# Rotary embedding without TensorE products: row-exchanged copies on ScalarE, cosine, sine and sum on GpSimd

## The chip, the cores and the metric

The kernel runs on one core of a Trainium2 chip. The metric is the device time of one execution in microseconds, lower is better. The engines are TensorE (PE in the rows, with its weight loads as PEld), VectorE (DVE), ScalarE (ACT), GpSimd (POOL) and SyncE (SP), which issues most of the transfers.

## The reference

Two transformer-like blocks on 256 tokens of width 1024, in float32. What matters here is the input projection of each block, and the rotary embedding of some of its columns:

```python
def rope(x, pos):                      # block one; _rope of block two is the same
    half = HEAD_DIM // 2               # 32
    ...
    x1, x2 = xf[..., :half], xf[..., half:]
    return jnp.concatenate([x1 * c - x2 * s, x2 * c + x1 * s], axis=-1)
...
# block one, beside an RWKV-7 recurrence over the same projection
z = u @ w_in[i]
qkv = z_attn.reshape(B, S, 3, N_GROUPS, ATTN_HEADS_PER_GROUP, HEAD_DIM)
q = rope(qkv[:, :, 0], pos)            # 768 columns
k = rope(qkv[:, :, 1], pos)            # 768 columns
# block two: rope on q_b, q_idx, q_c (256 columns each), k_b, k_idx, k_cmp, k_sel, k_win (64 each)
```

In block one q and k go into a dilated attention; RWKV-7 runs beside it. In block two the rotated columns go into a top-k attention, its index scores, and an attention with compressed, selected and windowed keys.

## The kernel before

All work is written out by hand, engine by engine. Five programs (`sync_program`, `tensor_program`, `scalar_program`, `vector_program`, `gpsimd_program`) walk through the same generators. A yield is a place where a `Turns` object switches between a main stream and a side stream; the order of each engine's instructions is fixed when the program is built. Engines meet only at semaphores: each `Count` (`rope_act`, `rope_pool`, ...) is one, `up(...)` raises it and `at(...)` is the value to wait for.

**Weights.** A stream (`st1` for block one, `st2` for block two) brings weight slots, 1 MB each as a rule, into a ring of three. The load of slot j waits until TensorE has finished slot j-3. Each product is made from a high and a low part: ScalarE writes the high part of a slot's two halves (`split(st, j, (0,))` and `split(st, j, (1,))`, rows `parts<-low 128x1024` on ACT), VectorE subtracts to get the low part (rows `parts<-low,parts` on DVE, line 2710), and TensorE waits for the low part (`parted`) of each half. With these parts it computes z by features, 256 columns a chunk (`feature_chunk`, lines 807, 808 and 816: 2 x 24 matmuls of 256 columns), or by tokens (`token_range`, lines 721 to 723). Feature chunks alternate between PSUM banks 0 and 1, and ScalarE reads a finished bank before the chunk after next may write it.

**Rotary embedding.** Here z of a chunk stands as features by tokens, 128 rows being two heads, so the partner of a row is 32 rows away. ScalarE copies z to SBUF (`rope_read`), TensorE multiplies the copy by the constant matrix `C_ROT` (ones and minus ones) one chunk later (`rotate`, line 766), and VectorE multiplies the product by sine (line 2783). In block one VectorE also makes the cosine product out of PSUM (line 2816) and the sum (line 2822). In block two GpSimd makes the cosine product (line 3701) and the sum (line 3706).

**Block one, chunks 10 to 15 of `st1`** are q and k, called n = 0 to 5. They are the main stream; RWKV is the side stream: `strict` (lines 1132 on TensorE, 2964 to 2971 on VectorE), then the levels of `chain` (lines 1192 to 1225 on TensorE, 3002 on VectorE, and copies out of PSUM on ScalarE). In order_1, between chunk n = 1 and chunk n = 2 TensorE has the first level's products (lines 1192, 1195, 1145), and within chunk n = 2 the products of line 1217. The scores of the attention (line 1346) wait for the last rotated chunk.

**Block two.** Plan n = 0 and 1 are head chunks without rotation. n = 2 to 6 are slots j = 0 to 4 of `st2`: n = 5 has four pieces of 64 columns, n = 6 has only 128 columns. Slots 5 and 6 hold 464 columns by tokens (`token_range`, `read_vt`), in five pieces each. That range writes first the bank of chunk n = 5 (token half i = 0), then the bank of chunk n = 6 (i = 1). After chunk n = 6 ScalarE copies rotated keys to other rows (`high<-high 64x256`, three of them), which waits for the sum of n = 5.

ScalarE's side of a chunk:

```python
for n in range(steps):
    if n < 2:
        split(st, j + 1, (n,))
    yield
q.wait_ge(*main_pe.at(st.tag, j, 1))
read()
yield
```

and `split` itself waits for the slot's transfer (`landed`) and for TensorE's end of slot j-2.

## Time and profile before

| | us |
|---|---|
| median of 3 runs | 912.58 (911.99 to 912.64) |
| the profiled execution, its own time | 912.49 |
| its span, first to last instruction | 910.7 |
| outside the span | 1.8 |
| TensorE busy in the span | 890.3 (98%) |
| VectorE busy | 604.7 (66%) |
| ScalarE busy | 454.3 (50%) |
| GpSimd busy | 44.3 (5%) |

The granted clock of TensorE is 0.998 of full speed (2.4 GHz) over the span. Busy time of TensorE counts pipelined matmuls, so a busy TensorE says that there is no gap, not that it runs at its peak. The chain that ended last says which engine's work set the end at each place.

### The profile page before, as it was taken

Reading aid. Unit: us, or ns where it says so; the run is one execution under the profiler, and the core shown is the slowest. Engines: PE = TensorE matmul, PEld = TensorE weight load, DVE = VectorE, ACT = ScalarE, POOL = GpSimd, SP = SyncE. Lnnn points to the kernel's source line nnn. Section 1 sums busy time; section 2 is a strip of 40 time slices with the busy share of each in tenths; the row PEclk is TensorE's granted clock in tenths of the full one; section 3 lists DMA queues with packets and bytes.
Section 4 is the critical chain, followed back from the end, with each engine's and each line's share of the span. In section 5 each row is a group of like instructions: output and inputs, shape, how many; then the busy total and the mean of one; then the engine's idle time right before and its main releaser. Section 6 shows DMA issues by size and latency. Waiting matters only on the chain.

```text
span 910.7 us, 15439 instructions
## 1 busy us (share of the span) xinstructions
PE 890.3 (98%) x6574; PEld 752.5 (83%) x6574; DVE 604.7 (66%) x966; ACT 454.3 (50%) x731; POOL 44.3 (5%) x61
## 2 busy tenths in 40 slices
PE   7999999999899999999999999999999999999997
PEld 5999988787789888888889978776788788888885
DVE  4577978557766666656766477877863566666673
ACT  4775444346443444546544356484622545555561
POOL 0010000010000000000000440000000000000000
PEclk9999999999999999999999999999999999999999
DMA  9544333233578665555339574353817566665521
GB/s 341 186 139 140 97 100 110 72 95 117 206 254 278 185 185 187 189 202 203 108 130 222 137 223 145 127 186 96 276 44 208 141 188 189 192 192 192 200 95 47
DMA packets 131205, 150.78 MB, mean 166 GB/s; under 512 B 11808, under 2 KB 102176, under 8 KB 131008
## 3 DMA queue, kind: packets, MB, share of 16 engines
q1 hardware_dynamic: 129920, 145.57, 51.6%
q10 hardware_dynamic: 1216, 4.23, 1.2%
q8 instruction: 52, 0.85, 0.4%
q14 instruction: 17, 0.14, 0.0%
HBM read 148.73 MB, written 1.05 MB: 164 GB/s over the span
## 4 chain that ended last, share of the span: by engine, by line
PE 90%; DVE 4%; ACT 2%; issue 2%; DMA 1%; POOL 0%; POOLq 0%; ACTq 0%; DVEq 0%
PE psum L834 12%; PE psum L721 10%; PE psum L723 9%; PE psum L722 9%; PE psum L839 7%; PE psum L807 4%; PE psum L808 4%; PE psum L816 4%; PE psum L787 4%; PE psum L727 3%; PE psum L883 2%; PE psum L893 2%; PE psum L884 2%; PE psum L840 2%; PE psum L1724 2%
## 5 line engine op out<-in xcount | busy, mean ns | idle before, releaser
L1827 ACT ACTIVATE parts<-low 128x1024 fp32r<-128x1024 f32 (+3 forms) x252 | 254.3, 1044 | 66.3 <-PE psum L723 50.2
L2710 DVE TENSOR_TENSOR parts<-low,parts 128x1024 fp32r<-128x1024 f32 (+3 forms) x156 | 187.9, 1234 | 27.6 <-ACT parts L1827 27.4
L721 PE MATMUL psum<-parts 128*128 128x512 f32 (+2 forms) x424 | 169.4, 399 | 1.8 <-DVE parts L2710 1.0
L723 PE MATMUL psum<-parts 128*128 128x512 f32 (+2 forms) x424 | 163.5, 386 | 0.0
L722 PE MATMUL psum<-parts 128*128 128x512 f32 (+2 forms) x424 | 163.4, 385 | 0.0
L1827 ACT ACTIVATE high<-psum 128x512 f32<-128x512 f32 (+4 forms) x95 | 52.4, 562 | 162.0 <-PE psum L840 76.4
L834 PE MATMUL psum<-parts 128*128 128x512 f32 x462 | 116.8, 392 | 0.0
L834 PEld LDWEIGHTS psum<-parts 128*128 128x128 f32 x462 | 86.9, 188 | 16.9
L721 PEld LDWEIGHTS psum<-parts 128*128 128x128 f32 x424 | 79.6, 188 | 23.3 <-issue 4.0
L723 PEld LDWEIGHTS psum<-parts 128*128 128x128 f32 x424 | 79.6, 188 | 16.3
L722 PEld LDWEIGHTS psum<-parts 128*128 128x128 f32 x424 | 79.8, 188 | 14.2 <-issue 0.2
L2775 DVE TENSOR_TENSOR parts<-low,parts 128x1024 fp32r<-128x1024 f32 x54 | 66.0, 1222 | 35.3 <-ACT parts L1827 35.3
L807 PE MATMUL psum<-parts 128*128 128x256 f32 (+2 forms) x312 | 82.3, 300 | 0.0
L808 PE MATMUL psum<-parts 128*128 128x256 f32 (+2 forms) x312 | 76.8, 282 | 0.0
L839 PEld LDWEIGHTS psum<-parts 128*128 128x128 f32 x528 | 72.0, 190 | 5.1
L839 PE MATMUL psum<-parts 128*128 128x256 f32 x528 | 73.6, 282 | 0.0
L807 PEld LDWEIGHTS psum<-parts 128*128 128x128 f32 (+2 forms) x312 | 58.9, 189 | 4.1 <-issue 3.2
L808 PEld LDWEIGHTS psum<-parts 128*128 128x128 f32 (+2 forms) x312 | 59.0, 189 | 2.3 <-issue 2.2
L3206 DVE TENSOR_TENSOR mid<-psum,high 128x512 f32<-128x512 f32 x33 | 22.8, 691 | 46.2 <-ACT high L1827 46.2
L816 PE MATMUL psum<-parts 128*128 128x256 f32 (+2 forms) x312 | 43.8, 283 | 0.0
L3669 POOL TENSOR_TENSOR low<-low 128x1 f32<-128x1 f32 x20 | 11.0, 550 | 632.3 <-DVE low L2634 316.2
L816 PEld LDWEIGHTS psum<-parts 128*128 128x128 f32 (+2 forms) x312 | 40.0, 189 | 0.1
(317 smaller groups left out, 1340.0 us busy)
## 6 DMA issues: line engine op xcount, KB each, us to landing
low<-in_w_in_dram SPq DMA_DIRECT2D x40, 1024.0 KB, 5.3
low<-in_w_ffn_in_dram SPq DMA_DIRECT2D x44, 512.0 KB, 5.2
low<-in_w_ff_in_dram SPq DMA_DIRECT2D x16, 1024.0 KB, 5.9
low<-in_w_ff_out_dram SPq DMA_DIRECT2D x16, 1024.0 KB, 4.9
low<-in_w_ffn_out_dram SPq DMA_DIRECT2D x11, 1024.0 KB, 4.9
low<-in_w_out_dram SPq DMA_DIRECT2D x8, 1024.0 KB, 5.3
low<-in_w_ple_gate_dram SPq DMA_DIRECT2D x4, 1024.0 KB, 4.9
low<-consts_dram ACTq DMA_DIRECT2D x1, 2142.0 KB, 9.0
```

What stands on the lines that cost most here:

```text
L721: mm(o, l[0], r[0], start, False)
L722: mm(o, l[0], r[1], False, False)
L723: return mm(o, l[1], r[0], False, stop)
L787: t = mm(PSUM[0:m, banks[n], 256 * j + 128 * i:256 * j + 128 * i + 128], w3[:, k, off:off + m], uT[:, k, 128 * i:128 * i + 128], k == 0, k ...
L807: mm(o, hi[:, k, c], st.uh[:, k, :], k == 0, False)
L808: mm(o, lo_[:, k, c], st.uh[:, k, :], False, False)
L816: t = mm(o, hi[:, k, c], st.ul[:, k, :], False, k == 7)
L834: mm(p, hi[:, k, c], st.u2(k), k == 0, False)
L839: mm(p[:, 0:256], lo_[:, k, c], st.uh[:, k, :], False, False)
L1827: return e.activation(o, a, ACT.Copy)
L2710: tt(rslot3(n, nk, width)[:, r, 0:w], slot3(n, nk, width)[:, r, 0:w], st.hi3(j)[:, r, 0:w].bitcast(F32), ALU.subtract) \
L2775: tt(rview(OR + 2048 * n + 1024 * (k % 2), 1024), slot(n)[:, 1024 * (k % 2):1024 * (k % 2) + 1024], rview(base, 1024).bitcast(F32), ALU.su ...
```

## The change

1. The constant `C_ROT` goes, and with it TensorE's rotation (`rotate`, line 766) of all eleven rotated chunks, and VectorE's products and sums (lines 2783, 2816, 2822).
2. ScalarE writes, besides the plain copy of z, a second copy with 32-row blocks exchanged (`swapped`: four copies of 32 rows out of PSUM) straight into the place of the result.
3. GpSimd multiplies the plain copy by cosine, the exchanged copy by sine (the sign now lies in the sine table) and adds them, in block one too. Its first product waits for the plain copy only.
4. ScalarE's copy of a chunk waits for GpSimd's sum of two chunks before; the bank comes free after the fourth exchanged copy; the scores of block one wait for GpSimd's last sum.
5. In block two the first half's split of slots 2 to 6 is issued right after the wait for the chunk's end and ahead of the chunk's copies (`ahead`), not behind them.

```diff
-            def rotate(tag, n, m, z):
-
-                b = 2 + n % 2 if tag == "qk" else 5 + n % 3
-                p = bank(b)
-                q.wait_ge(*rope_act.at(tag, n))
-                mm(p[:, 0:256 * m], const(C_ROT, 128), z, True, True).then_inc(rope_pe.up(tag, n), 1)
-                free[b] = [rope_dve.at(tag, n)]
...
-                        q.wait_ge(*rope_dve.at("qk", 5, "sum"))
+                        q.wait_ge(*rope_pool.at("qk", 5))
...
+            def ahead(st, j):
+
+                return st.tag == "st2" and 2 <= j <= 6
+
             def feature_chunk(st, j, widths, read):
                 steps = 1 + len(widths)
                 for n in range(steps):
-                    if n < 2:
+                    if n == 1 or n == 0 and not ahead(st, j + 1):
                         split(st, j + 1, (n,))
                     yield
                 q.wait_ge(*main_pe.at(st.tag, j, 1))
+                if ahead(st, j + 2):
+                    split(st, j + 2, (0,))
                 read()
                 yield
...
+            def swapped(dst, z):
+
+                for p in range(4):
+                    t = copy(dst[32 * p:32 * p + 32], z[32 * (p ^ 1):32 * (p ^ 1) + 32])
+                return t
+
-            def rope_read(tag, n, m, b, zs):
+            def rope_read(tag, n, m, b, zs, dst):
                 if n >= (2 if tag == "qk" else 4):
-                    q.wait_ge(*(rope_pe.at(tag, n - 2) if tag == "qk" else rope_pool.at(tag, n - 2)))
-                copy(zs, halves(bank(b))[:, 0:m, :]).then_inc(rope_act.up(tag, n), 1)
+                    q.wait_ge(*rope_pool.at(tag, n - 2))
+                z = halves(bank(b))[:, 0:m, :]
+                copy(zs, z).then_inc(rope_act.up(tag, n, "z"), 1)
+                swapped(dst, z).then_inc(rope_act.up(tag, n), 1)
...
-            def cosines(n, b):
-                q.wait_ge(*rope_act.at("qk", n))
-                tt(rt1[n % 2], halves(bank(b)), rep(const(C_COS, 256), 2), ALU.mult).then_inc(rope_dve.up("qk", n, "cos"), 1)
-
-            def rotate1(n):
-                dst = qk[:, 2 * n:2 * n + 2, :]
-                rotate("qk", n, 2, dst, const(C_SIN, 256))
-                q.wait_ge(*rope_dve.at("qk", n))
-                tt(dst, dst, rt1[n % 2], ALU.add).then_inc(rope_dve.up("qk", n, "sum"), 1)
...
-            def rope(tag, n, m, zs, t1, cos):
+            def rope(tag, n, m, zs, dst, cos, sin):
+                q.wait_ge(*rope_act.at(tag, n, "z"))
+                tt(zs, zs, rep(const(cos, 256), m), ALU.mult).then_inc(rope_pool.up(tag, n, "cos"), 1)
                 q.wait_ge(*rope_act.at(tag, n))
-                tt(t1, zs, rep(cos, m), ALU.mult).then_inc(rope_pool.up(tag, n, "cos"), 1)
-
-            def rotate(tag, n, dst, t1):
-                q.wait_ge(*rope_dve.at(tag, n))
-                q.wait_ge(*rope_pool.at(tag, n, "cos"))
-                tt(dst, dst, t1, ALU.add).then_inc(rope_pool.up(tag, n), 1)
+                tt(dst, dst, rep(const(sin, 256), m), ALU.mult).then_inc(rope_pool.up(tag, n, "sin"), 1)
+                q.wait_ge(*rope_pool.at(tag, n, "sin"))
+                tt(dst, dst, zs, ALU.add).then_inc(rope_pool.up(tag, n), 1)
```

**VectorE in block one**, from the end of `strict` to the second group of low parts (line numbers shift by 5 to 20 between the kernels). Before:

```order
61 L2971 TENSOR_TENSOR high<-high,low 64x512 x2
62 L2971 TENSOR_TENSOR mid<-high,low 64x512
63 L2971 TENSOR_TENSOR high<-high,low 64x512
64 L2816 TENSOR_TENSOR mid<-psum,low 128x512
65 L2783 TENSOR_TENSOR mid<-psum,low 128x512
66 L2822 TENSOR_TENSOR mid<-mid 128x512
67 L2710 TENSOR_TENSOR parts<-low,parts 128x1024 x2
68 L2816 TENSOR_TENSOR mid<-psum,low 128x512
69 L3002 TENSOR_TENSOR high<-psum,low 64x512 x4
```

Of the changed kernel, the same place:

```order
61 L2951 TENSOR_TENSOR high<-high,low 64x512 x2
62 L2951 TENSOR_TENSOR mid<-high,low 64x512
63 L2951 TENSOR_TENSOR high<-high,low 64x512
64 L2705 TENSOR_TENSOR parts<-low,parts 128x1024 x2
65 L2982 TENSOR_TENSOR high<-psum,low 64x512 x4
66 L2958 TENSOR_TENSOR high<-psum,low 128x4x128 x2
```

The low parts of the next slot now follow the four products of `strict` directly, and the products of the first level follow these.

**ScalarE in block one**, around chunks n = 0 and 1 (`mid<-psum 128x512` is the plain copy of q or k, `high<-psum` are RWKV's copies). Before:

```order
60 L1827 ACTIVATE mid<-psum 128x512
61 L1827 ACTIVATE parts<-low 128x1024
62 L1827 ACTIVATE high<-psum 128x512
63 L1827 ACTIVATE parts<-low 128x1024
64 L1827 ACTIVATE high<-psum 128x512
65 L1827 ACTIVATE mid<-psum 128x512
66 L1827 ACTIVATE parts<-low 128x1024 x2
```

Of the changed kernel:

```order
60 L1808 ACTIVATE mid<-psum 128x512
61 L1808 ACTIVATE mid<-psum 32x512 x4
62 L1808 ACTIVATE parts<-low 128x1024
63 L1808 ACTIVATE high<-psum 128x512
64 L1808 ACTIVATE parts<-low 128x1024
65 L1808 ACTIVATE high<-psum 128x512
66 L1808 ACTIVATE mid<-psum 128x512
67 L1808 ACTIVATE mid<-psum 32x512 x4
68 L1808 ACTIVATE parts<-low 128x1024 x2
```

Four copies of 32 rows stand between the plain copy and the next slot's splits.

**ScalarE in block two**, from the end of chunk n = 4 to the second token slot (`128x928` are halves of slots 5 and 6). Before:

```order
268 L1827 ACTIVATE high<-psum 128x512
269 L1827 ACTIVATE parts<-low 128x928 x2
270 L1827 ACTIVATE high<-psum 128x256
271 L1827 ACTIVATE high<-high 64x256 x3
272 L1827 ACTIVATE parts<-low 128x928 x2
```

Of the changed kernel:

```order
278 L1808 ACTIVATE parts<-low 128x928
279 L1808 ACTIVATE high<-psum 128x512
280 L1808 ACTIVATE high<-psum 32x2x256 x4
281 L1808 ACTIVATE parts<-low 128x928 x2
282 L1808 ACTIVATE high<-psum 128x256
283 L1808 ACTIVATE high<-psum 32x256 x4
284 L1808 ACTIVATE high<-high 64x256 x3
285 L1808 ACTIVATE parts<-low 128x928
```

The first halves of slots 5 and 6 now stand ahead of the copies of chunks n = 5 and n = 6; the second half of slot 5 stands behind five copies of n = 5 in place of one.

## Rows read from the trace of the kernel before

**Rows 1.** The page: busy time by engine.
```profile
PE 890.3 (98%) x6574; PEld 752.5 (83%) x6574; DVE 604.7 (66%) x966; ACT 454.3 (50%) x731; POOL 44.3 (5%) x61
```

**Rows 2.** Windows: busy us of each engine (instructions), clock, DMA share, GB/s.
```profile
84.00:100.00 16.00, 16.00 (x236) 15.10 (x235) 12.60 (x23) 8.13 (x13) 0.00 (x0) 1.00 0.43 133
100.00:112.00 12.00, 11.94 (x267) 10.70 (x266) 11.06 (x14) 4.66 (x7) 0.00 (x0) 1.00 0.29 90
112.00:152.00 40.00, 39.88 (x948) 34.99 (x948) 31.00 (x44) 16.89 (x26) 0.00 (x0) 1.00 0.35 108
500.00:532.00 32.00, 31.43 (x219) 28.32 (x218) 17.59 (x15) 12.76 (x19) 18.68 (x17) 1.00 0.72 193
```

**Rows 3.** Line 766, the rotations: min/median/max ns, first and last start.
```profile
L766 PE MATMUL psum<-mid,low x12: 590/590/594, 94.3 to 148.2; 128*128 128x512 f32 x12
L766 PE MATMUL psum<-high,low x10: 378/590/594, 502.9 to 527.1; 128*128 128x512 f32 x8, 128*128 128x256 f32 x2
```

**Rows 4.** The chain that ended last, pieces: start, us, what.
```profile
94.49 0.86 PE psum L766 x2
...
524.42 3.17 DVE parts L2710 x2
527.63 0.48 PE psum L721
```

**Rows 5.** Timeline of VectorE in block one: start, us, instruction.
```profile
95.79 1.41 DVE L2971 TENSOR_TENSOR high<-high,low 64x512 f32<-64x512 f32 x2
...
98.67 0.69 DVE L2816 TENSOR_TENSOR mid<-psum,low 128x512 f32<-128x512 f32 x1
...
100.60 2.35 DVE L2710 TENSOR_TENSOR parts<-low,parts 128x1024 fp32r<-128x1024 f32 x2
...
103.47 2.84 DVE L3002 TENSOR_TENSOR high<-psum,low 64x512 f32<-64x512 f32 x4
```

**Rows 6.** Timeline of TensorE in block one.
```profile
102.65 0.38 PE L807 MATMUL psum<-parts 128*128 128x256 f32 x1
...
106.55 0.27 PE L1217 MATMUL psum<-high 64*64 64x64 f32 x1
...
153.73 0.94 PE L1346 MATMUL psum<-mid 64*128 64x128 f32 x12
```

**Rows 7.** Timeline of ScalarE in block one.
```profile
93.10 0.60 ACT L1827 ACTIVATE mid<-psum 128x512 f32<-128x512 f32 x1 [4.65 <-PE psum L816]
93.59 1.05 ACT L1827 ACTIVATE parts<-low 128x1024 fp32r<-128x1024 f32 x1
...
100.57 0.60 ACT L1827 ACTIVATE mid<-psum 128x512 f32<-128x512 f32 x1 [2.28 <-PE psum L816]
...
145.31 0.60 ACT L1827 ACTIVATE mid<-psum 128x512 f32<-128x512 f32 x1 [1.98 <-PE psum L816]
...
151.37 2.31 ACT L1827 ACTIVATE high<-psum 64x512 f32<-64x512 f32 x4 [3.57 <-PE psum L1221]
```

**Rows 8.** Timeline of VectorE and GpSimd in block two.
```profile
502.29 1.28 POOL L3701 TENSOR_TENSOR high<-high,low 128x512 f32<-128x512 f32 x1 [15.90 <-ACT high L1827]
504.60 3.45 DVE L2710 TENSOR_TENSOR parts<-low,parts 128x1024 fp32r<-128x1024 f32 x2
504.68 2.30 POOL L3706 TENSOR_TENSOR high<-high 128x512 f32<-128x512 f32 x1 [1.11 <-DVE high L2783]
```

**Rows 9.** Timeline of ScalarE in block two.
```profile
501.61 0.60 ACT L1827 ACTIVATE high<-psum 128x512 f32<-128x512 f32 x1 [3.26 <-PE psum L816]
503.51 2.01 ACT L1827 ACTIVATE parts<-low 128x1024 fp32r<-128x1024 f32 x2 [1.30 <-DMA low<-in_w_in_dram]
...
521.92 1.84 ACT L1827 ACTIVATE parts<-low 128x928 fp32r<-128x928 f32 x2
525.15 0.38 ACT L1827 ACTIVATE high<-psum 128x256 f32<-128x256 f32 x1 [1.39 <-PE psum L816]
```

**Rows 10.** Timeline of SyncE: issue of slot 5's five pieces.
```profile
514.82 2.65 SPq L615 DMA_DIRECT2D low<-in_w_in_dram  x5
```

More of the change, by code:

```diff
@@ L20 @@
 S0 = math.exp(-0.5)
-C_ID, C_SU, C_IU, C_LI, C_ONE, C_BLK, C_ROT, C_M0, C_D64 = [128 * i for i in range(9)]
-C_LV = 128 * 9
+C_ID, C_SU, C_IU, C_LI, C_ONE, C_BLK, C_M0, C_D64 = [128 * i for i in range(8)]
+C_LV = 128 * 8
 C_MA = C_LV + 768
@@ L391, in program @@
         vtok = view3(P + 7168, 2, 768)
-        rz1 = [view3(P + 8704 + 1024 * i, 2, 256) for i in range(2)]
         rt1 = [view3(P + 9216 + 1024 * i, 2, 256) for i in range(2)]
@@ L438, in program @@
         rz2 = [view3(P + 23080 + 1024 * i, 2, 256) for i in range(2)]
-        rt2 = [view3(P + 23592 + 1024 * i, 2, 256) for i in range(2)]
         oC = view3(P, 6, 256)
@@ L572, in program @@
         main_pe, main_act, main_dve, main_pool = [count("main_" + n) for n in ("pe", "act", "dve", "pool")]
-        rope_pe, rope_act, rope_dve, rope_pool = [count("rope_" + n) for n in ("pe", "act", "dve", "pool")]
+        rope_act, rope_pool = [count("rope_" + n) for n in ("act", "pool")]
         rw_pe, rw_act, rw_dve, rw_pool = [count("rwkv_" + n) for n in ("pe", "act", "dve", "pool")]
@@ L1003, in qkv @@
                 for n in range(6):
-                    yield from feature_chunk(st1, QK_AT + n, next(pg), [128, 128], [rope_dve.at("qk", n, "cos")],
-                                             (lambda n=n: rotate("qk", n - 1, 2, rz1[(n - 1) % 2])) if n else nothing)
+                    yield from feature_chunk(st1, QK_AT + n, next(pg), [128, 128], [rope_act.at("qk", n)], nothing)
             def gate(r, late):
@@ L1011, in gates @@
                 for r in (2, 3, 0, 1):
-                    yield from gate(r, (lambda: rotate("qk", 5, 2, rz1[1])) if r == 2 else nothing)
+                    yield from gate(r, nothing)
             rw_bank = itertools.cycle((4, 5, 6, 7))
@@ L1908, in token_range @@
                         for r in range(nk // 2):
-                            if i == 0 and r < 2:
+                            if i == 0 and (r == 1 or r == 0 and not ahead(st, j0 + s + 1)):
                                 split(st, j0 + s + 1, (r,))
@@ L2005, in qkv @@
                     b = next(pg)
-                    yield from feature_chunk(st1, QK_AT + n, [128, 128], lambda: rope_read("qk", n, 2, b, rz1[n % 2]))
+                    yield from feature_chunk(st1, QK_AT + n, [128, 128], lambda: rope_read("qk", n, 2, b, rt1[n % 2], qk[:, 2 * n:2 * n + 2, :]))
             def gate(r):
@@ L2830, in qkv @@
                 for n in range(6):
-                    b = next(pg)
-                    yield from feature_chunk(st1, QK_AT + n, [128, 128], lambda: cosines(n, b), (lambda n=n: rotate1(n - 1)) if n else nothing)
+                    next(pg)
+                    yield from feature_chunk(st1, QK_AT + n, [128, 128], nothing, nothing)
             def gate(r, late):
@@ L2838, in gates @@
                 for r in (2, 3, 0, 1):
-                    yield from gate(r, (lambda: rotate1(5)) if r == 2 else nothing)
+                    yield from gate(r, nothing)
             rw_bank = itertools.cycle((4, 5, 6, 7))
@@ L3295, in vector_program @@
             st2 = ST["st2"]
-            def rotate2(n):
-                if n >= 2:
-                    rotate("in2", n, 1 if n == 6 else 2, rope_to(n), const(C_SINC if n == 6 else C_SIN, 256))
-            turns.beside(head("in2", st2, nothing, lambda n: rotate2(n - 1)), seam_ple(1), 3)
+            turns.beside(head("in2", st2, nothing, nothing), seam_ple(1), 3)
             def read_vt(i, p):
@@ L3317, in main_b @@
                     next(pg)
-                    yield from feature_chunk(st2, n - 2, plan_2[n][1], nothing, lambda: rotate2(n - 1))
-                yield from token_range(st2, 5, 2, read_vt, lambda: rotate2(6))
+                    yield from feature_chunk(st2, n - 2, plan_2[n][1], nothing, nothing)
+                yield from token_range(st2, 5, 2, read_vt, nothing)
             turns.alone(main_b())
@@ L3737, in qkv @@
                 for n in range(6):
-                    yield from feature_chunk(st1, QK_AT + n, [128, 128], nothing, nothing)
+                    yield from feature_chunk(st1, QK_AT + n, [128, 128], lambda: rope("qk", n, 2, rt1[n % 2], qk[:, 2 * n:2 * n + 2, :], C_COS, C_SIN), nothing)
             def gate(r, late):
```

33 lines of the change are left out of this document (10 added, 23 removed).

## The prediction

> **What bounds the kernel now.** The page's busy times come first: TensorE is busy 98% of the span, GpSimd 5% [rows 1]. The windows then show the two places of the change: in block one TensorE is busy for 67.8 of the 68 us from 84 to 152, in block two 31.4 of 32 us [rows 2]. The reader is to see that work off TensorE counts only if it delays TensorE, and that VectorE has 11.06 busy us of 12 between 100 and 112, against 31.0 of 40 afterwards [rows 2]. The rotations themselves are 12 and 10 instructions, two to each chunk, so six and five products [rows 3], and the chain of waits gives 0.86 us of its own time to a pair [rows 4]. Last, the timelines tell how late each low part may be.
>
> **What goes.** In block one six pairs on TensorE, 6 x 0.86 = 5.2 us. In block two four wide pairs and one half as wide (0.378 us an instruction against 0.590 [rows 3], so some 0.6 us), 4.0 us together. The first number, 9.2 us, is what a reader would take who looks at TensorE alone. VectorE loses 18 operations in block one and five in block two, of 0.69 us each [rows 5]; its time is not on the path except where it makes low parts.
>
> **What comes on ScalarE.** Four copies of 32 rows a chunk. No row shows this form. A 128-row copy out of PSUM takes 0.60 us, and its successor starts 0.49 after it [rows 7]; four of 64 rows took 2.31, that is 0.57 apart [rows 7]. The nearest form is the copy before them, same bank and same columns, so I take 0.49 apart, 1.96 us for four; the other end is 0.57, 2.3 us. Less than 0.49 would need a copy to be cheaper for having fewer rows, and 64 rows were no cheaper. The copies lie beside TensorE's work: in block one ScalarE is busy 16.9 of 40 us [rows 2], and a chunk with its share of RWKV lasts 11.2 us (100.57 to 145.31 is four [rows 7]). Without that cover each would cost 0.5. In block two a chunk will last 5.75 us (6.61 before, less 0.86), and ScalarE's list for it is 0.5 + 1.96 + 2.0 of splits [rows 7, 9]: it fits, with little room.
>
> **What comes on GpSimd, and what it takes from VectorE.** Three products of 1.28 us a chunk where it had none in block one and two in block two [rows 8]. This is where I see the price. At 504.60 two low parts took 3.45 us; the same two take 2.35 elsewhere [rows 5, 8]. GpSimd's sum began at 504.68 and took 2.30, not 1.28 [rows 8]. Laid side by side: VectorE's first until 505.8, GpSimd until 507.0, VectorE's second until 508.05. So they alternate whole instructions, and each GpSimd product put in between delays VectorE by 1.1 to 1.15 us. The rows show this for the low parts (both inputs in SBUF) only. The Trainium skill, page "SBUF — State Buffer", section "SBUF: two separate sides", states it as an exclusive lock: a VectorE operation with two SBUF inputs and a GpSimd operation that reads SBUF exclude each other for a whole instruction. By that rule line 2971 meets it and the products out of PSUM (line 3002) don't; with it the sum is the one below, and by the low parts alone it is that of the first rival.
>
> *Block one, the dense place.* Chunk n = 0 is copied at 93.10; its exchanged copies end at 95.6, so GpSimd's sine product is there at 95.7, its sum at once behind it. VectorE starts the four products of line 2971 at 95.79 and ends them at 98.64, since line 2816 follows at 98.67 [rows 5]. I take line 2971 to meet the products as the low parts do: + 2 x 1.15, end 100.9. The end of chunk n = 1 comes 0.86 earlier, at 99.7; its plain copy is done at 100.3 and the cosine product waits from 100.4, ahead of VectorE's next. It runs 100.9 to 102.1; first low part 102.1 to 103.3; sine (there at 102.3) to 104.4; second low part to 105.6. TensorE's chunk n = 2 began at 102.65 [rows 6] and would now want its low parts at 101.8 and, 8 matmuls of 0.12 later, at 102.75. It waits 1.5 for the first and 1.35 for the second (103.3 + 0.96 = 104.3, so until 105.6): 2.85 us. What is late next: line 3002 runs 105.6 to 108.4 (before 103.47 to 106.31 [rows 5]); TensorE comes to line 1217 at 106.55 - 1.72 + 2.85 = 107.7 [rows 6], its first half is ready at 107.0 and the second, needed at 108.8, at 108.4. No further wait. Later chunks have VectorE's slack (31.0 of 40 busy, less 2.0 a chunk that is removed, plus at most 3.5), so they keep their 0.86. Lower end of this cost: if line 2971 doesn't meet GpSimd, its low parts start at 98.65 and are done at 101.0, and TensorE never waits: 0. Upper end: one more product in between, 4.0.
> Block one: -5.2 + 2.85 = **-2.3** (-5.2 to -1.2).
>
> The scores wait for the last sum now. Chunk 5's copy, 145.31 before [rows 7], comes at 145.31 - 5 x 0.86 + 2.85 = 143.9; sums follow within 6.3 us, at 150.2. The scores stood at 153.73 [rows 6], now at 151.4. Hidden by 1.2 us; each microsecond beyond would cost one.
>
> *Block two, ScalarE in order.* Slot 2's split stood behind the copy of chunk j = 0 at 501.61 and waited for its transfer until 503.51 [rows 9]. Now the copies stand behind it, with what is queued there: plain copy 504.5 to 505.0, exchanged to 507.0, second split to 508.05. GpSimd's sine holds VectorE until 508.35, so the second low part comes at 509.5. TensorE wants it at 508.1 (chunk 2 starts 507.15): 1.4 us lost. Chunk 3 then starts at 514.35, chunk 4 at 520.1 (1.15 ahead of before).
> Slot 5 was issued at 514.82 in five pieces over 2.65 us [rows 10], and ScalarE took it at 521.92 without a wait [rows 9], so it landed within 7.1 us of its first issue; as the chunk's end before it moves up by 0.3 only, I take 6.5 to 7.1. ScalarE: split of slot 5 from 521.1 to 522.0, copies to 524.5, second half to 525.4; the low part, with GpSimd's sine ahead of it, at 526.8. TensorE resumed here at 527.63 [rows 4], held then by two low parts that took 3.17 in the chain [rows 4].
> Then slot 6's first split stands ahead of the copies of n = 6. Issued at 520.3 it lands at 526.8 by the same 6.5; split to 527.7, narrow copies (0.38 each [rows 9], some 0.27 apart) to 529.1. TensorE may write the bank of n = 6 (token half i = 1) only then. Before, it came to i = 1 at 527.63 + 6 x 0.21 = 528.9. So all five rotations of block two are spent on waits: **0** (-1.2 if slot 6 lands 1 us sooner and line 816's end is followed directly; -2.7 if ScalarE were never held; +1 if both slots need 7.1).
>
> **Sum.** -2.3 + 0 against the profiled execution's own 912.49 us (span 910.7 and 1.8 around it) gives 910.2; the median of the runs is 0.09 above that execution, which I ignore. The 128 columns of constants that go, 64 KB of one transfer, I cost at nothing: they load beside weights; if they were on the path they would give 0.2.
>
> **Rivals.**
> 1. *The engines don't meet outside the low parts.* For: the rows show only these. Then block one gives its 5.2 whole: 912.49 - 5.2 + 0 = **907.3**. Chance 0.25. With block two unhindered too (transfers in time, -2.7): **904.6**, chance 0.08.
> 2. *ScalarE is held longer in block two.* 0.57 apart adds 0.35 to the wait in chunk 2 and again at the end, and slots at 7.1 us add 0.6 to 0.9: +1.3 together, **911.5**. For: slot 2 did make it wait [rows 9]. Chance 0.12.
> 3. *Copies that change rows are dear, slower than before.* At 1.1 us apart ScalarE's list for a chunk of block two is 0.5 + 4.4 + 2 = 6.9, over TensorE's 5.75. The wait in chunk 2 grows by 4 x 0.61 = 2.4; the copies of n = 5 add 2.4 again, less the 1.4 that ScalarE stands before slot 6 anyway (525.4 to 526.8); the narrow ones add 1.3: + 4.8 us at the bank of n = 6, **915.0**. It decides from about 1.04 us apart, where the time passes 914.4. Against: no row here has a copy of 512 columns out of PSUM above 0.60 [rows 7, 9]. Chance 0.10.
>
> **How the numbers follow.** My forecast, 910.2, has 0.45. Outside 906 to 913 lie the unhindered case (0.08) and the third rival (0.10), hence that range; the forecast's own range is 909 to 911.3. A change of 0.2%, 1.8 us, is about what a measurement of this kernel can tell from none: faster means under 910.76. Of the forecast's 0.45 I count 0.29 faster and 0.16 the same; the first rival is faster (0.33), the second the same (0.11, 0.01 slower), the third slower. Faster 0.62, same 0.27, slower 0.11.
>
> **What would show it.** No line 766 on TensorE. Of block one: line 2971's successors (low parts) beginning near 101 and not 98.7, TensorE idle for 1 to 3 us in chunk n = 2 with VectorE as releaser, none in chunks 3 to 5. GpSimd products of 1.28 alone and about 2.3 beside two-input operations. Four copies of 32 rows in about 2.1 us. Of block two: ScalarE waiting on transfers ahead of slots 2, 5 and 6; TensorE waiting once in chunk 2 and again in slot 5's range, the second time for ScalarE. I am wrong if TensorE shows no wait in block one, or if a wait stands where I see none, at the scores above all.

## The result, and the profile after

The changed kernel takes 913.83 us (median of 20 runs, 912.87 to 916.90) beside 912.53 for the kernel before on the same chip (20 runs, 911.90 to 913.73). The ratio is 1.0018, interval 1.0012 to 1.0024: slower, by 1.3 us in the medians, which is less than the 1.8 that I had called measurable. I had forecast 910.2 in a range of 906 to 913, with faster as the likeliest; the time lies outside that range and on the other side of the kernel before.

Fifteen of its 20 runs lie between 913 and 914.7 us, but the profiled execution took 916.7 (span 914.9) and a second one 915.9; a part of this difference is the granted clock, as the windows below show.

The page of the changed kernel, busy time by engine, answers to [rows 1]:

```profile
PE 884.8 (97%) x6552; PEld 751.0 (82%) x6552; DVE 596.1 (65%) x943; ACT 480.7 (53%) x775; POOL 78.0 (9%) x84
```

The windows of the changed kernel, columns as in [rows 2]:

```profile
84.00:100.00 16.00, 16.00 (x265) 15.54 (x268) 12.59 (x19) 10.90 (x18) 4.50 (x3) 1.00 0.43 133
100.00:112.00 12.00, 8.98 (x233) 8.20 (x223) 11.31 (x11) 6.80 (x11) 4.92 (x3) 1.00 0.29 90
112.00:152.00 40.00, 38.91 (x955) 35.60 (x954) 25.09 (x32) 27.21 (x42) 15.78 (x12) 1.00 0.35 108
500.00:532.00 32.00, 27.05 (x190) 25.79 (x190) 11.74 (x9) 20.71 (x31) 19.96 (x13) 0.89 0.65 165
```

TensorE, which had next to no idle time in [rows 2], is idle for 3.0 us between 100 and 112, 1.1 us between 112 and 152, and 4.95 us in block two, where its granted clock is 0.89 too. The rotations are gone (22 matmuls fewer), and waits stand in their place.

VectorE, GpSimd and TensorE at the dense place of block one in the changed kernel (start, us, instruction, and in brackets the idle time before it and its releaser):

```profile
95.90 2.38 DVE L2951 TENSOR_TENSOR high<-high,low 64x512 f32<-64x512 f32 x2
98.31 1.67 DVE L2951 TENSOR_TENSOR mid<-high,low 64x512 f32<-64x512 f32 x1
100.01 0.69 DVE L2951 TENSOR_TENSOR high<-high,low 64x512 f32<-64x512 f32 x1
100.73 4.41 DVE L2705 TENSOR_TENSOR parts<-low,parts 128x1024 fp32r<-128x1024 f32 x2
105.06 2.84 DVE L2982 TENSOR_TENSOR high<-psum,low 64x512 f32<-64x512 f32 x4
```
```profile
96.15 1.59 POOL L3679 TENSOR_TENSOR mid<-mid,low 128x512 f32<-128x512 f32 x1 [1.06 <-ACT mid L1808]
...
100.35 1.48 POOL L3677 TENSOR_TENSOR mid<-mid,low 128x512 f32<-128x512 f32 x1 [0.91 <-ACT mid L1808]
...
104.13 2.15 POOL L3681 TENSOR_TENSOR mid<-mid 128x512 f32<-128x512 f32 x1
```
```profile
103.06 0.36 PE L794 MATMUL psum<-parts 128*128 128x256 f32 x1 [1.24 <-DVE parts L2705]
...
103.96 0.28 PE L795 MATMUL psum<-parts 128*128 128x256 f32 x1
105.19 0.39 PE L794 MATMUL psum<-parts 128*128 128x256 f32 x1 [0.95 <-DVE parts L2705]
105.41 0.28 PE L795 MATMUL psum<-parts 128*128 128x256 f32 x1
...
108.04 0.24 PE L1203 MATMUL psum<-high 64*64 64x64 f32 x1 [0.67 <-DVE high L2982]
...
140.79 0.24 PE L1203 MATMUL psum<-mid,high 64*64 64x64 f32 x1 [0.20 <-DVE mid L2972]
...
153.42 0.94 PE L1332 MATMUL psum<-mid 64*128 64x128 f32 x12
```

Lines 2951, 2705, 2982, 794 and 1203 are the former 2971, 2710, 3002, 807 and 1217. The first two products of line 2951 take 2.38 us instead of 1.41 [rows 5], the third 1.67 instead of 0.69 (a single one takes 0.69, as the fourth does here), and the pair of low parts 4.41 instead of 2.35. TensorE waits for each low part and then for line 2982. The scores start at 153.42, only 0.3 earlier than in [rows 6].

ScalarE and TensorE in block two of the changed kernel:

```profile
504.99 1.06 ACT L1808 ACTIVATE parts<-low 128x1024 fp32r<-128x1024 f32 x1 [6.92 <-DMA low<-in_w_in_dram]
505.96 2.99 ACT L1808 ACTIVATE high<-psum 128x512 f32<-128x512 f32 x5
508.97 2.00 ACT L1808 ACTIVATE parts<-low 128x1024 fp32r<-128x1024 f32 x2
...
525.53 3.01 ACT L1808 ACTIVATE high<-psum 128x512 f32<-128x512 f32 x5
...
530.30 0.98 ACT L1808 ACTIVATE parts<-low 128x928 fp32r<-128x928 f32 x1 [0.74 <-DMA low<-in_w_in_dram]
```
```profile
509.00 0.39 PE L794 MATMUL psum<-parts 128*128 128x256 f32 x1 [1.95 <-ACT high L1808]
511.44 0.58 PE L794 MATMUL psum<-parts 128*128 128x256 f32 x1 [0.94 <-DVE parts L2705]
528.60 0.47 PE L716 MATMUL psum<-parts 128*128 128x464 f32 x1 [1.23 <-ACT high L1808]
530.94 0.48 PE L716 MATMUL psum<-parts 128*128 128x464 f32 x1 [0.82 <-DVE parts L2705]
533.30 0.47 PE L716 MATMUL psum<-parts 128*128 128x464 f32 x1 [0.83 <-ACT high L1808]
...
543.82 1.14 PE L1548 MATMUL psum<-high 64*128 64x256 f32 x8
```

Five copies out of PSUM, one plain and four of 32 rows, take 3.0 us (1.95 for the half as wide ones of n = 6). Three of TensorE's five waits end with the last of such a batch ("ACT high": the bank is free only then), two with a low part. They add up to 5.77 us, against 0.56 in the kernel before. The first scores of block two start at 543.82; in the kernel before this row reads

```profile
539.41 1.13 PE L1567 MATMUL psum<-high 64*128 64x256 f32 x8
```

From the scores of block one to these is 390.40 us, against 385.68 before: + 4.7. From there to the end of the own time it is 372.9 against 373.1. So the 4.2 us between the two profiled executions are - 0.3 in block one, + 4.7 in block two, and - 0.2 behind them.

Windows of the changed kernel around its second wait in block two (PEclk is the third number from the end):

```profile
510.00:516.00 6.00, 5.06 (x24) 4.76 (x23) 4.41 (x3) 4.99 (x8) 5.91 (x4) 0.50 0.04 11
...
517.00:523.00 6.00, 6.00 (x52) 6.00 (x51) 0.76 (x2) 4.12 (x7) 3.00 (x3) 1.00 0.56 144
```

After the waits of 1.95 and 0.94 us the granted clock is at its lower level, 1.2 GHz, for over six microseconds: 24 matmuls take 5.06 busy us where 52 take 6.00, so about 2.3 us are lost by the clock alone.

So of the + 4.7 in block two the waits make 5.2, the clock 2.3, and the rotations that are gone give back 4.0: + 3.5. The other 1.2 are not resolved one by one; a part of it is what a wait costs beyond its idle time, of which more below.

### The profile page after: what moved, and what is told of

It reads as the page before. It is cut to its first block, busy times and chain, and to the rows that moved or that the text cites. A ratio compares the mean times of both kernels' runs of the same rounds, so it can differ in the third digit from the quotient of the medians.

```text
span 914.9 us, 15437 instructions
## 1 busy us (share of the span) xinstructions
PE 884.8 (97%) x6552; PEld 751.0 (82%) x6552; DVE 596.1 (65%) x943; ACT 480.7 (53%) x775; POOL 78.0 (9%) x84
## 4 chain that ended last, share of the span: by engine, by line
PE 81%; DVE 8%; ACT 4%; DMA 3%; issue 2%; SPq 2%; POOL 0%; POOLq 0%; ACTq 0%; DVEq 0%
PE psum L821 12%; PE psum L716 9%; PE psum L718 9%; PE psum L717 9%; PE psum L826 7%; PE psum L794 3%; PE psum L722 3%; PE psum L795 3%; PE psum L803 3%; PE psum L870 2%; PE psum L880 2%; PE psum L871 2%; PE psum L774 2%; DVE parts L2705 2%; PE psum L827 2%
## 5 line engine op out<-in xcount | busy, mean ns | idle before, releaser
L2705 DVE TENSOR_TENSOR parts<-low,parts 128x1024 fp32r<-128x1024 f32 (+3 forms) x156 | 191.4, 1254 | 49.0 <-ACT parts L1808 48.8
L1808 ACT ACTIVATE high<-psum 128x512 f32<-128x512 f32 (+6 forms) x115 | 63.3, 559 | 130.6 <-PE psum L827 76.4
L794 PEld LDWEIGHTS psum<-parts 128*128 128x128 f32 (+2 forms) x312 | 60.1, 193 | 8.0 <-DVE parts L2705 2.4
L795 PEld LDWEIGHTS psum<-parts 128*128 128x128 f32 (+2 forms) x312 | 60.2, 193 | 0.3 <-issue 0.3
L1808 ACT ACTIVATE mid<-psum 32x512 f32<-32x512 f32 (+7 forms) x61 | 32.9, 552 | 31.8 <-PE psum L803 12.9
```

Source lines behind the costliest of these rows:

```text
L794: mm(o, hi[:, k, c], st.uh[:, k, :], k == 0, False)
L795: mm(o, lo_[:, k, c], st.uh[:, k, :], False, False)
L1808: return e.activation(o, a, ACT.Copy)
L2705: tt(rslot3(n, nk, width)[:, r, 0:w], slot3(n, nk, width)[:, r, 0:w], st.hi3(j)[:, r, 0:w].bitcast(F32), ALU.subtract) \
```

## The experiments

All times are medians, each beside the kernel before on the same chip (912.5 to 912.9). "The changed kernel" is the 913.83 above. Line numbers shift by some lines from kernel to kernel, and the code excerpts are cut.

**e1: block one alone.** The kernel before, with the change in block one only (copies exchanged on ScalarE, three products on GpSimd; block two keeps its rotations and order).

> Block one as changed, block two as before (rotations on TensorE there). The trace of the changed kernel has TensorE at the scores of block one 0.3 us ahead of before and at the first scores of block two 4.4 us behind. Theory 'block two loses, block one gives almost nothing': 912.2 us (911.6 to 912.8), no measurable change. Rival 'block one loses too, its profiled execution was a good one': 913.5 us or more.

Measured: 912.10 (911.05 to 913.70), ratio 0.9995 (0.9986 to 1.0003). As expected, with the same two waits for low parts (1.24 and 0.94 us). The waits of 0.67 and 0.16 behind them are absent: the granted clock had fallen to 0.50 between 105 and 108, and TensorE came that much later. The 5.2 us of rotations in block one bring 0.6 by the medians, and the interval does not exclude nothing.

**e2: block two's splits behind the copies again.**

```diff
-                return st.tag == "st2" and 2 <= j <= 6
+                return False
```

> The changed kernel with block two's first-half splits back behind the copies, as in the kernel before (the fifth part of the change undone). Theory 'the splits put ahead make ScalarE stand before the transfers of slots 2 and 6 while finished banks wait behind it': the waits for a bank in chunk 2 (1.95 us) and for the bank of n = 6 (0.83 us) go, a wait for slot 5's low part grows by up to 1 us: about 911.5 us (910.5 to 912.5). Rival 'the four exchanged copies themselves are too much for ScalarE there, in any order': 913.8 us, no change against the changed kernel.

Measured: 913.01 (911.87 to 914.27), ratio 1.0008 (0.9999 to 1.0017): 0.8 under the changed kernel, a third of what I expected and outside my range; the runs of the two overlap. The bank waits went (1.95 us in chunk 2, 1.23 and 0.83 at slots 5 and 6), but the low part of slot 5 now stood behind the batch of copies. ScalarE and TensorE in e2:

```profile
519.67 3.02 ACT L1808 ACTIVATE high<-psum 128x512 f32<-128x512 f32 x5 [1.56 <-PE psum L803]
```
```profile
525.16 0.45 PE L716 MATMUL psum<-parts 128*128 128x464 f32 x1 [2.38 <-DVE parts L2705]
```

One order makes the bank late, the other the split: the 3 us of copies are in the way of one of the two.

**e3: banks of their own for the rotated chunks.** The later rotated chunks of block two use banks 7, 5 and 6, so that no matmul waits for ScalarE to free a bank.

```diff
+        def own_bank(n, b):
+            return {4: 7, 5: 5, 6: 6}.get(n, b)
...
-                    yield from feature_chunk(st2, n - 2, next(pg), plan_2[n][1], read2(n), nothing)
+                    yield from feature_chunk(st2, n - 2, own_bank(n, next(pg)), plan_2[n][1], read2(n), nothing)
```

> The changed kernel, but in block two chunks n = 4, 5 and 6 write banks 7, 5 and 6, so that neither chunk 2 nor the token range waits for a bank that ScalarE has still to copy. Theory 'the bank waits only come first; the low parts of the second half are as late behind them': the bank wait of chunk 2 goes but TensorE then waits for the second half's low part until the same moment, and only the last bank wait (0.83 us) is a gain: 913.0 us (912.5 to 913.5). Rival 'the bank is what costs': 2.8 us and more are gained, 911 us or less.

Measured: 918.07 (915.13 to 919.40), ratio 1.0055 (1.0044 to 1.0067): a miss by 5 us. The bank waits are gone, but TensorE was held by the low parts instead, now in one piece each: in chunk 2 until 511.29 where the changed kernel had 511.44, in slot 5 until 529.84 where it had 530.94. TensorE and windows in e3:

```profile
511.29 0.58 PE L798 MATMUL psum<-parts 128*128 128x256 f32 x1 [2.56 <-DVE parts L2709]
```
```profile
509.00:514.00 5.00, 2.71 (x12) 2.71 (x13) 3.52 (x2) 4.89 (x8) 4.92 (x3) 0.69 0.36 103
...
530.00:534.50 4.50, 4.50 (x15) 3.89 (x16) 1.79 (x2) 4.24 (x10) 4.42 (x6) 0.65 0.84 334
```

After each of the two long waits (2.56 and 2.30 us) the clock fell. Five of its six runs have a mean granted clock of 0.992 to 0.994 and take 916.9 to 919.4; the sixth has 0.999 and took 915.13. Even that sixth run is 1.3 us above the changed kernel. Removing a wait whose successor is nearly as late won nothing here, and the runs spent more time at the low clock.

**e4: GpSimd's first products of block one held back.** The changed kernel, with one wait more on GpSimd.

```diff
             def rope(tag, n, m, zs, dst, cos, sin):
+                if (tag, n) == ("qk", 0):
+                    q.wait_ge(*rw_dve.at("T", 1, 1, 1))
```

> The changed kernel, but in block one GpSimd's first product (and with it all of chunks n = 0 and 1) waits for VectorE's last product of the chain's first level, so that GpSimd is silent while VectorE makes the four products of line 2951 and slot 12's low parts. Theory 'GpSimd takes VectorE's turns there': the waits of 1.24, 0.95, 0.67 and 0.16 us and their restarts go, a gain of 3.0 to 3.5 us against the changed kernel: 910.5 us (909.8 to 911.2). Rival 'TensorE waits there because ScalarE's high parts come 3 us later': no change, 913.8 us.

Measured: 911.99 (909.93 to 914.46), ratio 0.9994 (0.9985 to 1.0003), 1.8 under the changed kernel; the profiled execution took 909.93, and the scores of block one start at 150.63, 2.8 earlier than in the changed kernel. All four waits of the dense place are gone. The median is over my range, and the clock goes with it: the five runs with a granted clock of 0.998 or more took 909.9 to 911.3, the six others 912.0 to 914.5. Where it fell in those six is not shown; the profiled execution has 0.999. TensorE of e4:

```profile
150.63 0.94 PE L1332 MATMUL psum<-mid 64*128 64x128 f32 x12
...
504.47 0.39 PE L794 MATMUL psum<-parts 128*128 128x256 f32 x1 [0.24 <-ACT high L1808]
506.91 0.39 PE L794 MATMUL psum<-parts 128*128 128x256 f32 x1 [1.23 <-DVE parts L2705]
...
537.00 1.13 PE L1548 MATMUL psum<-high 64*128 64x256 f32 x8
```

This execution also shows block two of the changed kernel without a fall of the clock: 386.37 us between the two scores, only 0.7 more than before.

**e5: e1 with that wait.** Block one changed and held back, block two as before.

> Block one has the change, and GpSimd's products of the first two rotation chunks wait for VectorE's last product of line 2971's group there, so VectorE meets none of them in the dense place; block two is as before. Theory (VectorE and GpSimd take turns at the dense place, and block two's part of the change gives nothing): TensorE's four waits in chunk n = 2 and behind it go, which is 3.0 us against e1_block1_only (912.1): 909.1, range 908.4 to 909.8, and VectorE's first low part of that place takes 2.4 us for the pair, not 4.4. With no long waits in one stretch the granted clock should stay at its high level and the runs should lie within 1 us of each other. Rival (block one's loss was something else, as the stalls that name no releaser): no more than 1 us under e1, 911 or more.

Measured: 909.24 (908.50 to 909.77), ratio 0.9961 (0.9949 to 0.9974), 2.9 under e1. VectorE of e5:

```profile
96.08 1.40 DVE L2983 TENSOR_TENSOR high<-high,low 64x512 f32<-64x512 f32 x2
97.51 0.69 DVE L2983 TENSOR_TENSOR mid<-high,low 64x512 f32<-64x512 f32 x1
...
98.95 2.36 DVE L2722 TENSOR_TENSOR parts<-low,parts 128x1024 fp32r<-128x1024 f32 x2
```

With GpSimd silent, each of these is back at its duration before the change, and as work and data are the same, what made them longer is the contention. No run of e5 is as slow as the fastest of e1. e5 is also 2.75 under e4, which differs from it only in block two: there the change costs, it does not merely fail to pay. At a granted clock of 0.998 or more the difference is 1.7 (e4 910.9, e5 909.24); the rest goes with the clock.

**e6: one plain copy for the four exchanged ones in block two.** The exchange is left out there, so block two's rotated q and k are not the reference's.

```diff
+                if tag == "in2":
+                    copy(dst, z).then_inc(rope_act.up(tag, n), 1)
+                    return
                 swapped(dst, z).then_inc(rope_act.up(tag, n), 1)
```

> The changed kernel, but in block two the four copies of 32 rows that exchange the row blocks are one plain copy of all 128 rows, so the exchange is left out there and block two's rotated q and k are not the reference's. ScalarE then has 0.5 us where it had about 2.4 in each chunk. Theory (ScalarE's time is what holds the bank and the low parts of block two): the waits at the banks of n = 5 and n = 6 and at the low parts go, except what slot 2's transfer causes; TensorE's sum in block two falls by 2.5 to 4 us and the time is 910 to 911.3. Rival (VectorE's low parts under GpSimd's three products hold block two): the waits stay, 913 or more.

Measured: 911.43 (910.75 to 912.51), ratio 0.9987 (0.9978 to 0.9996), 2.4 under the changed kernel and 0.1 over my range. Waits in block two fall from 5.8 us to 2.5. ScalarE's copies are the larger part of the loss, and not all of it. ScalarE of e6, two plain copies of 128 rows:

```profile
505.47 1.07 ACT L1808 ACTIVATE high<-psum 128x512 f32<-128x512 f32 x2
```

**e7: e4 and e2 together.**

> e4_gpsimd_late with block two's splits back behind the copies, as in e2_no_ahead. If the two gains add (1.8 from the wait of GpSimd, 0.8 from the splits' place) the median is 911.2; if e2's gain was only the place in which the clock fell, the two are the same, 912.0. Range 910.4 to 912.2. The wait of about 2.4 us at the low part of slot 5 is expected to stand here too.

Measured: 910.25 (909.54 to 911.56), ratio 0.9975 (0.9965 to 0.9985). The gains of the two add, and somewhat more (3.6 us for 1.8 and 0.8), so that the median is 0.15 under my range. The wait for slot 5's low part stands, with 2.38 us as in e2; behind it the clock fell here and not in e2.

**e8: exchange later, out of SBUF.** This stands on e7. At a chunk's end ScalarE makes the plain copy alone; the four exchanging copies follow in the next chunk behind both splits and read that copy. GpSimd's products start after them.

```diff
                 copy(zs, z).then_inc(rope_act.up(tag, n, "z"), 1)
+                if tag == "in2":
+                    def exchange():
+                        q.wait_ge(*rope_act.at(tag, n, "z"))
+                        swapped(dst, zs).then_inc(rope_act.up(tag, n), 1)
+                    pending.append(exchange)
+                    return
```

> As e7_late_no_ahead, but in block two ScalarE only copies the bank plainly at a chunk's end, which frees it; the four exchanging copies come in the middle of the next chunk, behind both splits, and read the plain copy in SBUF; GpSimd does all three products after them. Theory (block two's waits come from the 3 us of copies that stand between TensorE and its next split or bank): no wait over 0.5 us in block two but that for slot 2's transfer, so its 4.0 us are kept but for 1 us at most: 912.5 - 4.4 - 3.0 = 905.1, with the stalls of no releaser 906; range 905 to 908. Rival (GpSimd's products hold VectorE's low parts wherever they stand): low parts are still late by 1.2 us or more in three or more chunks, 909 to 911.

Measured: 917.39 (916.66 to 919.84), ratio 1.0050 (1.0037 to 1.0064): both theories missed, through two waits that I had overlooked. TensorE still waited for the exchanged copies before it wrote a bank again, though they no longer read it, and ScalarE's three small key copies wait for GpSimd's sum of n = 5, which had moved. ScalarE and TensorE of e8:

```profile
529.58 1.30 ACT L1808 ACTIVATE high<-high 64x256 f32<-64x256 f32 x3 [3.57 <-POOL high L3695]
530.90 1.84 ACT L1808 ACTIVATE parts<-low 128x928 fp32r<-128x928 f32 x2
```
```profile
534.51 0.76 PE L716 MATMUL psum<-parts 128*128 128x464 f32 x1 [6.08 <-ACT high L1808]
```

The wait of 3.57 us on ScalarE holds the split of slot 6 behind it. A step moved later moves every wait on its result.

**e9: both mended.** The excerpt is against e8; the token range also has one place more at which ScalarE takes up the copies put off.

```diff
-                return [main_act.at("qa", n) if n < 2 else rope_act.at("in2", n)]
+                return [main_act.at("qa", n) if n < 2 else rope_act.at("in2", n, "z")]
...
-                    if n == 6:
-                        q.wait_ge(*rope_pool.at("in2", 5))
+                    if n == 6:
+                        def keys():
+                            q.wait_ge(*rope_pool.at("in2", 5))
...
+                        pending.append(keys)
```

> e8_late_deferred with the two faults that its trace shows mended: TensorE's wait for a bank of block two is for the plain copy and not for the exchanged ones, and ScalarE's three key copies, which wait for GpSimd's last wide sum and held the split of slot 6, stand behind that split. Theory (ScalarE's copies ahead of what TensorE waits for are the whole of block two's loss): TensorE's waits in block two fall to under 1.5 us together, of which the transfers' share is the larger, and the time is 905.3 to 907. Rival (GpSimd's products delay the low parts of block two wherever they stand): waits for low parts of 0.5 to 1.2 us in two or more chunks, 907.5 to 909.

Measured: 908.59 (908.01 to 909.21), ratio 0.9957 (0.9943 to 0.9971). The waits in block two are 2.6 us, four of the five of them for low parts (0.77 the longest), and it is the rival that comes true: VectorE of e9, the low parts of slot 3,

```profile
507.34 4.20 DVE L2719 TENSOR_TENSOR parts<-low,parts 128x1024 fp32r<-128x1024 f32 x2 [2.88 <-ACT parts L1808]
```

**e10: the changed kernel again, one profiled execution.**

> The changed kernel again, for a second profiled execution. By the theory its four waits in block one stand at the same places with the same sizes within 0.1 us, since instructions set them; in block two the wait at slot 2 moves with the landing of that transfer, and the granted clock may or may not fall around 510. If the clock doesn't fall there, the time is 912.9 to 913.5 instead of 914 or more.

Measured: 915.92. The waits for low parts at the dense place are 1.25 and 0.96 us, those of block two 2.06, 1.24, 1.23, 0.82 and 0.79: the same places. The clock fell in block two again, and now in block one as well, and the third and fourth wait there (0.67 and 0.16) are absent. Windows of e10:

```profile
105.00:108.00 3.00, 3.00 (x14) 3.00 (x15) 2.88 (x5) 0.00 (x0) 1.07 (x1) 0.50 0.00 0
```

Between 105 and 108 the changed kernel's first profiled execution had a clock of 1.00, after waits of the same size to 0.01 us. In block one this fall cost nothing: TensorE, slower, came to the next products when they were ready, and the scores start at 153.47 beside 153.42.

**e11: e9 with block two's products on VectorE**, three of 0.69 us behind both low parts of a chunk, and none on GpSimd.

> e9_deferred_freed with block two's three products of each chunk on VectorE, behind both of its low parts, and none on GpSimd. By e9's trace a pair of low parts takes 4.2 us there when GpSimd multiplies and 2.36 when it doesn't. Theory (GpSimd's products are the other half of block two's loss): the waits for low parts go, block two's waits fall from 2.6 us to under 1.2, the three products take VectorE about 2.1 us a chunk in its own slack, and the time is 907.0 to 907.9. Rival (the low parts are late because ScalarE's high parts are, with the transfers): the waits stand, 908.4 or more.

Measured: 908.19 (907.12 to 909.20), ratio 0.9951 (0.9938 to 0.9965). The low parts of the same slot in e11,

```profile
508.97 2.35 DVE L2719 TENSOR_TENSOR parts<-low,parts 128x1024 fp32r<-128x1024 f32 x2
```

and no wait for a low part is over 0.4 us. But one wait of 2.03 us had appeared: by the timelines TensorE wanted the bank of token half 0, which VectorE read last, behind the products of n = 6 and its three key copies. So the waits of block two still add up to 2.6 us, not to under 1.2, and the time lies between my two ranges; the 0.4 us to e9 are within the spread of five runs. The products on VectorE show in the durations of the low parts, and not yet in the time.

**e12: e11 with the key copies moved.** The excerpt is against e11. VectorE's last products and key copies go half a slot earlier, ScalarE's key copies behind the next split.

```diff
-                            if (i, r) in ((0, 1), (1, 0)) and pending:
+                            if (s, i, r) in ((0, 0, 1), (1, 0, 1)) and pending:
...
-                yield from token_range(st2, 5, 2, read_vt, nothing)
+                yield from token_range(st2, 5, 2, read_vt, nothing, keys)
```

> e11_products_on_vector with the last chunk's products and VectorE's three key copies half a slot earlier, ahead of the reading of the range's first bank, and ScalarE's three key copies half a slot later, behind the split that they held. In e11 TensorE's one long wait of block two, 2.03 us, ended when VectorE had read that bank, behind products and key copies. Theory (it is this order): the wait falls to under 0.5 us and the time to 906.2 to 907.2. Rival (the moved work delays the low part ahead of it and only shifts the wait): 907.8 or more.

Measured: 906.04 (904.74 to 906.78), ratio 0.9924 (0.9910 to 0.9938). It is faster than the kernel before by 6.6 us and than the changed one by 7.8. The wait is 0.97 us now, not under 0.5, and the time came out 0.2 under my range all the same. TensorE of e12:

```profile
533.90 1.13 PE L1548 MATMUL psum<-high 64*128 64x256 f32 x8
```

Block two's first scores stand 5.5 us ahead of the kernel before (539.41), of the 9.2 us that the rotations took.

## Why the prediction was wrong

**The contention in block one: right.** I took line 2971 to meet GpSimd's products, and two products to delay it. It took 0.97 and 0.98 us longer, the low parts 2.06. e5 shows it by undoing it alone. The products out of PSUM (line 2982) kept the 2.84 us of [rows 5], though GpSimd's sum (104.13 to 106.28) ran beside the first of them. Both agree with the rule of the Trainium skill, page "SBUF — State Buffer", section "SBUF: two separate sides", that the prediction had drawn on. The waits for low parts were 1.24 and 0.95 where I said 1.5 and 1.35.

**"No further wait" at line 1217: wrong, but small.** I had the two halves of line 3002 free TensorE in turn. It waited until 108.04, when all four products of the line were done (105.06 + 2.84 = 107.90), 0.67 us, and 0.16 more behind it. By the code it must: line 1217's first group writes the two PSUM banks that all four products read, which I had not looked at. Together the four waits are 3.0 us; that this is almost my 2.85 is luck, since two are shorter than I said and two I did not have.

**"Later chunks keep their 0.86": the step of block one that failed.** With 3.0 us of waits the scores should have come 2.2 earlier, and they came 0.3 earlier. Three things fill the gap. First, two stalls of TensorE inside groups of small matmuls (0.35 and 0.54 us, at 120.4 and 141.3) for which the profile names no releaser; the kernel before has none there, while e4 and e5 have such stalls at the same groups. Second, 0.20 us at 140.6 in which TensorE waits for VectorE's copy of line 2972. Third, a wait costs more than its idle time, because matmuls overlap: without the wait of 0.95 us the two behind 103.96 would have started at 104.08 and 104.20 (0.12 apart, as their neighbours), and they started at 105.19 and 105.41, the second 1.21 late. That is 0.26 more than the idle time. I took waits at their idle time in both blocks; at 0.1 to 0.26 for each of the seven waits and stalls an estimate is 0.7 to 1.8 us, enough for the remaining 0.8. With the four waits gone the scores of e4 stood at 150.63, so 5.2 us of rotations are worth 3.1 there.

**"So all five rotations of block two are spent on waits: 0": the step that decided.** I had the waits of block two use up the 4.0 us of rotations and no more. In the profiled execution they are 5.77 us, 5.2 more than before, and the clock took 2.3 us on top, so that block two came out at + 4.7 and not at 0. ScalarE was held longer, as my second rival had it, but the cost was above the 1.3 us that I gave it. Two terms were off, and a third was not, though it looks like one.
- *The copies.* I took 0.49 us apart and gave 0.57 as the other end. The batch takes 3.02 us for five, 0.605 apart. So the batch is 0.5 longer than my sum, each time it stands ahead of TensorE.
- *The transfer of slot 2.* I left its landing at 503.51 [rows 9] and had the rest follow. It landed at 504.99 here. In chunk 2 I had 1.4 us of waiting; TensorE waited 1.95 for the bank and then 0.94 for the second low part. A landing that I read from one execution was no constant: the kernel before, e5 and e1 have the same block two, and slot 2 landed 1.90, 2.61 and 3.65 us behind the start of ScalarE's copy there. In e4's execution it landed at 500.46, as far behind the scores of block one as in the kernel before (349.8 us), and there the waits of chunk 2 are 0.24 + 1.23 = 1.47 us, my 1.4, and block two costs + 0.7, near my 0.
- *The low parts under GpSimd's three products.* I counted one of them in front of a low part, and they are not what decided in the changed kernel. The two low parts that TensorE waited for took 1.32 and 1.30 us,

```profile
510.06 1.32 DVE L2705 TENSOR_TENSOR parts<-low,parts 128x1024 fp32r<-128x1024 f32 x1 [2.75 <-ACT parts L1808]
...
529.59 1.30 DVE L2705 TENSOR_TENSOR parts<-low,parts 128x928 fp32r<-128x928 f32 x1 [2.92 <-ACT parts L1808]
```

against 1.23 and 1.13 for others of their size there; they were late because ScalarE's high parts were. Only in e9, with ScalarE's part of the loss mended, did TensorE wait for a pair that took 4.20 us.

e6 prices the four exchanging copies at 2.4 us. e11 and e12 take the products off GpSimd: by then no wait for a low part is over 0.4 us, and it is e12 that turns this into time.

**The clock: no term of mine.** The first profiled execution lost 2.3 us to it in block two, and the median lies 2.9 under that execution. The mean clock of a run does not order the times strictly (three runs with 0.996 took 913.1 to 913.7). And it isn't all: the eleven runs of the changed kernel with a clock of 0.998 or more have a median of 913.76, still 1.2 over the kernel before. So the sign does not rest on the clock; the wider spread (4 us against 1.8) goes with it.

**The rivals.** The first (contention only in low parts) is refuted by the rows of line 2951. The third (dear copies) is refuted as worked out, since it needed 1.04 us apart; it was the only one on the side on which the result fell, and the time came out there by another route, waits for ScalarE that I had priced under the second. The two ends I allowed around block two, - 2.7 and + 1, did not hold what came: + 4.7 in the profiled execution, and some + 1.5 by the runs at the high clock (1.2 over before, and 0.3 gained in block one). The range broke with them. The scores of block one did not wait for GpSimd's last sum, and the later stages took what they had taken (372.9 us against 373.1), as predicted.

## What to carry to other kernels

Work that is moved to an idle engine still has to be priced at its place in that engine's queue: here 3 us of copies stood between TensorE and its next bank or split, and whichever of the two was put first, the other was late (the changed kernel and e2). Before a helper's work is placed beside VectorE's two-input operations, ask for a stretch where VectorE has slack: one wait on GpSimd was worth 2.9 us (e5 against e1). When a result is made later, list all that waits for it and for its buffer; e8 lost 8.8 us against e9 by two such waits and the lower clock that came with them (0.992 to 0.994 in its runs, 0.998 to 1.000 in e9's). And count a wait at more than its idle time.

## What the runs showed of the hardware

- Behind TensorE's waits at the dense places the granted clock fell to its lower level (1.2 GHz) in some executions and not in others, with waits of the same size (at 105 in e1, e2 and e10, not in the changed kernel's first profiled execution); it stayed there for 3 to 7 us. The fall at 510 cost 2.3 us, those at 105 nothing by the scores of e2 and e10 (153.26 and 153.47, beside 153.42 without one). Far from the change it came in e12 behind a wait of 1.78 us, where the changed kernel waits 1.60 and has no fall:

```profile
229.87 0.50 PE L1395 MATMUL psum<-parts 128*128 128x512 f32 x1 [1.78 <-ACT mid L1804]
```
```profile
230.00:234.00 4.00, 4.00 (x11) 3.17 (x12) 3.97 (x6) 3.74 (x5) 0.00 (x0) 0.57 1.05 394
```

- A copy of 32 rows by 512 on ScalarE takes as long as one of 128 rows (0.60 us out of PSUM), and in a batch it is dearer: these copies start 0.605 us apart, where plain copies of 128 rows start 0.49 apart (two in 1.07 us, e6) and those of 64 rows 0.57 [rows 7]. Out of SBUF four take 2.54 (e8). Whether the few rows or their exchange keeps them apart, no run here separates.
- A VectorE product of two SBUF inputs and a GpSimd product delay each other, by up to an instruction: 64x512 went from 0.69 to 1.67 us, a pair of 128x1024 from 2.35 to 4.41, and GpSimd's 1.28 to 2.15 (104.13 above).
- With the rotations gone TensorE had short stalls (0.24 to 0.83 us) with no releaser in the profile, in groups of 64x64 matmuls of block one: two to four in each profiled execution of the changed kernel and of e1, e4, e5 and e7, and none in that of the kernel before. Their cause stays open; no run here varied it.
